# Matmuls whose result nobody reads at TensorE's waits, a merged last expert at the layer seam, and expert weights in 8 KB rows, in a two-layer hybrid MoE step

## The reference, cut to what matters

```python
def trunk_layer(x, cond, attend, p, w_router, router_bias):
    mod = jax.nn.silu(cond) @ p['w_ada'] + p['b_ada']
    sh1, sc1, g1, sh2, sc2, g2 = jnp.split(mod, 6, axis=-1)
    mix, k, v = mixer(modulate(x, p['norm1'], sh1, sc1), p, attend)
    x = x + g1 * mix
    h = modulate(x, p['norm2'], sh2, sc2)
    x = x + g2 * moe(h, w_router, router_bias, p['w_e_gate'], p['w_e_up'], p['w_e_down'])
...
def moe(h, w_router, router_bias, w_gate, w_up, w_down):
...
    # 16 experts in 4 groups; the best group, and its best 2 experts, are chosen for each token
    hid = jax.nn.silu(jnp.einsum('td,edf->tef', t, w_gate)) * jnp.einsum('td,edf->tef', t, w_up)
    hid = hid * combine.astype(hid.dtype)[..., None]
    return jnp.einsum('tef,efd->td', hid, w_down).reshape(B, L, D)
```

## Time and profile before

| | |
|---|---|
| median of 3 runs | 1215.33 us (1215.15 to 1216.3) |
| the profiled execution | 1213.5 us |
| its span (what the profile covers) | 1211.7 us |
| PE busy | 1114.1 us, 92% of the span |
| DVE, ACT, POOL busy | 699.8, 457.5, 58.0 us |
| chain that ended last, by engine | PE 68%, DVE 21%, ACT 4%, DMA 3%, issue 3% |
| mean granted TensorE clock | 0.971 of full speed |

### The profile page before, as it was taken

The page is one execution under the profiler, slowest core; times in us unless marked ns, Lnnn a source line. Parts: engine busy times, 40 slices in busy tenths (PEclk is TensorE's granted clock), DMA queues, the critical chain, the costliest instruction groups (busy, mean ns, idle before and its releaser), DMA issues.

```text
span 1211.7 us, 19456 instructions
## 1 busy us (share of the span) xinstructions
PE 1114.1 (92%) x6494; PEld 776.4 (64%) x6495; DVE 699.8 (58%) x1364; ACT 457.5 (38%) x827; POOL 58.0 (5%) x71
## 2 busy tenths in 40 slices
PE   3899999999898999999869999999998999999993
PEld 1798777678673455555459887776886655445551
DVE  0466999875632334445465799987654345234546
ACT  2443776443341122222254267645442222112224
POOL 1000000000100000000310000000000000000006
PEclk9999999999999999999979999999988999999996
DMA  8832655623798989999943446563058799989991
GB/s 316 272 109 104 215 206 209 239 72 105 296 395 314 345 312 395 393 394 395 386 134 107 141 170 235 201 218 115 3 187 301 272 392 394 392 278 395 395 374 54
DMA packets 138055, 309.93 MB, mean 256 GB/s; under 512 B 7953, under 2 KB 40113, under 8 KB 131329
## 3 DMA queue, kind: packets, MB, share of 16 engines
q1 hardware_dynamic: 134448, 302.25, 68.6%
q0 software_dynamic: 1472, 4.52, 1.0%
q10 hardware_dynamic: 2064, 2.22, 0.6%
HBM read 307.10 MB, written 1.87 MB: 255 GB/s over the span
## 4 chain that ended last, share of the span: by engine, by line
PE 68%; DVE 21%; ACT 4%; DMA 3%; issue 3%; DVEq 0%; SPq 0%; ACTq 0%
PE ps L772 15%; PE ps L805 11%; DVE conv L1878 7%; PE ps L775 6%; PE ps L859 5%; PE ps L906 3%; PE ps L1110 3%; PE ps L907 3%; PE ps L908 3%; PE ps L830 3%; DMA ring<-in_w_ada 2%; DVE w_lo L1894 2%; PE ps L831 2%; PE ps L1023 2%; PE ps L1025 2%
## 5 line engine op out<-in xcount | busy, mean ns | idle before, releaser
L1753 DVE SCALAR_TENSOR_TENSOR nat<-ps,weight,nat 128x512 f32<-128x512 f32 x180 | 124.1, 745 | 111.1 <-PE ps L831 111.1
L1878 DVE SCALAR_TENSOR_TENSOR conv<-ub,dw,conv 128x414 f32<-128x414 f32 x240 | 137.1, 645 | 0.1
L908 PE MATMUL ps<-h_hi,w_lo 128*128 128x384 f32 x384 | 130.4, 340 | 0.0
L1740 DVE TENSOR_TENSOR orow_lo<-ps,orow_hi 64x512 fp32r<-64x512 f32 (+1 forms) x64 | 44.1, 689 | 108.2 <-ACT orow_hi L1284 107.3
L772 PE MATMUL ps<-second,xgT 128*64 128x256 f32 x896 | 102.3, 381 | 0.0
L772 PE MATMUL ps<-ring,xgT 128*64 128x256 f32 x832 | 95.7, 381 | 1.4 <-DMA ring<-in_w_e_gate 1.0
L772 PEld LDWEIGHTS ps<-second,xgT 128*64 128x64 f32 x896 | 65.2, 137 | 39.0 <-issue 12.6
L906 PE MATMUL ps<-h_hi,gate_hi 128*128 128x384 f32 x256 | 90.0, 352 | 0.0
L907 PE MATMUL ps<-h_lower,gate_hi 128*128 128x384 f32 x256 | 87.1, 340 | 0.0
L772 PEld LDWEIGHTS ps<-ring,xgT 128*64 128x64 f32 x832 | 62.6, 137 | 36.5 <-issue 12.4
L1271 ACT ACTIVATE hidT<-ps 128x256 f32<-128x256 f32 (+1 forms) x32 | 13.4, 418 | 185.5 <-PE ps L790 185.5
(11 more groups left out here) (271 smaller groups left out, 2038.4 us busy)
## 6 DMA issues: line engine op xcount, KB each, us to landing
ring<-in_w_ada SPq DMA_DIRECT2D x48, 1024.0 KB, 7.4
second<-in_w_e_gate SPq DMA_DIRECT2D x32, 1024.0 KB, 11.7
second<-in_w_e_up SPq DMA_DIRECT2D x32, 1024.0 KB, 12.7
second<-in_w_e_down SPq DMA_DIRECT2D x32, 1024.0 KB, 11.7
ring<-in_w_e_gate SPq DMA_DIRECT2D x32, 1024.0 KB, 13.3
ring<-in_w_e_up SPq DMA_DIRECT2D x32, 1024.0 KB, 13.9
ring<-in_w_e_down SPq DMA_DIRECT2D x32, 1024.0 KB, 13.3
ring<-in_w_in SPq DMA_DIRECT2D x30, 1024.0 KB, 5.6
```

The source lines that it names most:

```text
L908: last = pe.matmul(ps[:, b, 0:T], lower[:, o:o + P], hi[:, k, 0:T], start=False, stop=(k == k_tiles - 1))
L1740: dve.tensor_tensor(orow_lo[a:z, o:o + 512], ps[a:z, 5 + h, :], orow_hi[a:z, o:o + 512].bitcast(F32), ALU.subtract).then_inc(fr[5 + h], 1)
L1753: dve.scalar_tensor_tensor(sums, ps[:, b, :], weight[:, t, bass.ds(at, 1)], sums, ALU.mult, ALU.add).then_inc(fr[b], 1)
L1878: dve.scalar_tensor_tensor(conv[:, i, :], src, w, conv[:, i, :], ALU.mult, ALU.add).then_inc(tapped, 1)
```

## The change

1. **Rows of 8 KB.** The expert weights' view is `(h p k) n` instead of `(k p) n`: partition p of a piece gets neighbouring rows of the matrix, one run of 8 KB. So that the products stay the same, the tokens are stored in the order that fits: ACT's `nat_hi` and DVE's `nat_lo` read PSUM in steps of 4 words, and DVE's `hid` reads silu (SBUF) and the up product (PSUM) in steps of 2 words.
2. **`stay_busy(b, n)`**: n bf16 matmuls of 128x512 into a bank, whose result nobody reads, ahead of a step that waits: 11 before `qkv` (layer 0), 5 before the first `scores`, 10 before `rank` (layer 1), 8 and 14 before `spread` (layers 0 and 1), and 2, 4 and 6 at the seam.
3. **Seam.** The body of expert 15 holds its last `back` and the question about overflow itself; one conditional jump and one jump are left. `n1` starts with banks 7 and 4.
4. **Order.** ACT's load of the sigmoid table (L1456) moves behind the modulation; `spread` does the three `nat_hi` products first, then the three of `nat_lo`; `lower_h(4)` moves behind the third pair of `place`.
5. In `add_routed` the factor 1.0 becomes a column of ones in SBUF.

```diff
-    ("n1", [0, 1, 7, 4, 0, 1]),
+    ("n1", [7, 4, 0, 1, 7, 4]),
...
+        def by_row(rows, t, h):
+            return rows[:, t, h * 512:(h + 1) * 512].rearrange("q (k p) -> q k p", k=4)
...
-        w_g = A["w_e_gate"].rearrange("l e (k p) n -> (l e) p k n", p=P)
+        w_g = A["w_e_gate"].rearrange("l e (h p k) n -> (l e) h p k n", h=2, p=P)
...
+            def stay_busy(b, n):
+
+                for _ in range(n):
+                    pe.matmul(ps[:, b, :], ones_b[:], ones_b[:].unsqueeze(1).to_broadcast([P, 4, P]), start=True, stop=True)
...
+                if l == 0:
+                    b, n = use("qkv", 0, l)
+                    begin(b, n)
+                    pe.wait_ge(consts2, 5)
+                    stay_busy(b, 11)
...
+                b, n = use("scores", 0, l)
+                begin(b, n)
+                stay_busy(b, 5)
                 scores(0)
...
-                pe.wait_ge(route_r, l + 1)
                 b, n = use("rank", 0, l)
                 begin(b, n)
+                if l + 1 == DEPTH:
+                    stay_busy(b, 10)
+                pe.wait_ge(route_r, l + 1)
...
+                        t, lower = i % NT, i // NT
+                        part = (nat_hi, nat_lo)[lower]
...
+                b, n = use("spread", 0, l)
+                begin(b, n)
+                hb, hn = use("h2n", 1, l)
+                pe.wait_ge(freed[hb], hn + 1)
+                stay_busy(b, 8 if l + 1 < DEPTH else 14)
...
+                                ahead = pe.mark_branch_hint_location()
+                                steps(small, before_narrow)
+                                last_back(small)
+                                pe.br_cond(over > 0, f"further{n}", f"usual{n}_{int(small)}")
+                                with nc.body(f"usual{n}_{int(small)}", valid_engines=[pe.engine]):
+                                    no_further()
+                                    pe.br(f"joined{n}").branch_hint(ahead)
...
+                    back(n_of, freed, full, small, range(0, 2))
+                    if l + 1 < DEPTH:
+                        stay_busy(3, 2)
+                    back(n_of, freed, full, small, range(2, NT), halves=(0,))
+                    if l + 1 < DEPTH:
+                        stay_busy(3, 4)
+                    back(n_of, freed, full, small, range(2, NT), halves=(1,))
...
+                    if l + 1 < DEPTH:
+                        stay_busy(3, 6)
...
-                act.activation(warm[:], eps[:], ACT.Sigmoid)
                 modulate("n2", 1, 1, l)
                 modulate("n2", 1, 2, l)
+                act.activation(warm[:], eps[:], ACT.Sigmoid)
...
-                    act.activation(nat_hi[:, t, h * 512:(h + 1) * 512], ps[:, b, :], ACT.Copy).then_inc(nat_hi_r, 1)
+                    act.activation(by_row(nat_hi, t, h), ps[:, b, :].rearrange("q (p k) -> q k p", k=4), ACT.Copy).then_inc(nat_hi_r, 1)
...
-                        dve.scalar_tensor_tensor(x_, routed[:, h, :], 1.0, x_, ALU.mult, ALU.add).then_inc(signal, 1)
+                        dve.scalar_tensor_tensor(x_, routed[:, h, :], ones[:, 0:1], x_, ALU.mult, ALU.add).then_inc(signal, 1)
...
-                dve.tensor_tensor(hid[:, 0:cols], silu[:, 0:cols], ps[:, 3, 0:cols], ALU.mult).then_inc(fr[3], 1)
+                    rows, pairs = "q (k p) -> q k p", "q (p k) -> q k p"
...
+                dve.tensor_tensor(hid[:, 0:cols].rearrange(rows, k=2, p=P), silu[:, 0:cols].rearrange(pairs, k=2, p=P),
+                                  ps[:, 3, 0:cols].rearrange(pairs, k=2, p=P), ALU.mult).then_inc(fr[3], 1)
...
-                        if half_at == 0 and t == NT - 1:
-                            lower_h(4)
...
-                        for i in (2, 3, 5):
+                        for i in (4, 2, 3, 5):
```

More of the change, by code:

```diff
@@ L817, in expert_parts, with back @@
                 return gate, up, turn_own, turn_hid, down
-            def back(n_of, fr, fs, small, tiles=range(NT), gate_bank=2):
+            def back(n_of, fr, fs, small, tiles=range(NT), gate_bank=2, halves=(0, 1)):
                 if 0 in tiles:
@@ L825, in back @@
                 for t in tiles:
-                    for h in range(2):
+                    for h in halves:
                         b, u = SUM_BANKS[2 * t + h]
@@ L1103, in spread @@
                     for i in range(2 * NT):
[L1104 to L1108, removed]
+                        t, lower = i % NT, i // NT
+                        part = (nat_hi, nat_lo)[lower]
+                        if half_at == 0 and k % 4 == 0:
+                            hi_ = H2N.index((t, k // 4))
+                            if lower:
+                                hb, hn = use("h2n", hi_, l)
+                                pe.wait_ge(freed[hb], hn + 1)
+                            else:
+                                pe.wait_ge(nat_hi_r, l * 6 + (hi_ + 1))
+                        if k == 0 and not lower:
                             pe.wait_ge(place_r, l * (2 * NT) + (half_at * NT + t + 1))
@@ L1130, in _, with expert @@
                 settle(pe)
-                def expert(e, before_e=None, in_second=False, turn=0, between=None):
+                def expert(e, before_e=None, in_second=False, turn=0, between=None, over=None):
                     if in_second:
@@ L1164, in steps @@
                         down(small)
-                    if before_e is None:
+                    if over is not None:
+                        narrow = pe.value_load(narrow_e[0:1, bass.ds(e, 1)], min_val=0, max_val=1)
+                        before_narrow = pe.value_load(narrow_e[0:1, bass.ds(before_e, 1)], min_val=0, max_val=1)
+                        n = next(forks)
+                        pe.br_cond(narrow > 0, f"small{n}", f"wide{n}")
+                        for small in (True, False):
+                            with nc.body(("wide", "small")[small] + str(n), valid_engines=[pe.engine]):
+                                ahead = pe.mark_branch_hint_location()
[5 more added lines that the diff above has]
+                                    pe.br(f"joined{n}").branch_hint(ahead)
+                        with nc.body(f"further{n}", valid_engines=[pe.engine]):
+                            further()
+                            pe.br(f"joined{n}")
+                        nc.switch_bb(f"joined{n}")
+                    elif before_e is None:
                         by_width(pe, e, steps)
@@ L1205, in further @@
                         back(lambda b: further_use(b, l, i), freed_o, full_o, False, range(NT), 5)
-                usual_or_over(pe, ahead, no_further, further)
+                expert(0, in_second=True, between=spread_rest)
+                with pe.Fori(0, NE // 2 - 1) as pair_:
+                    expert(pair_ * 2 + 1, pair_ * 2, False, pair_)
+                    expert(pair_ * 2 + 2, pair_ * 2 + 1, True, pair_ + 1)
+                over = pe.value_load(overfull[0:1, 0:1], min_val=0, max_val=1)
+                expert(NE - 1, NE - 2, False, NE // 2 - 1, over=over)
         @block.scalar
```

32 lines of the change are left out of this document (13 added, 19 removed).

## The result

The changed kernel took 1202.79 us (median of 4 runs, 1201.35 to 1203.38) where the kernel before took 1215.47: a ratio of 0.9913, with an interval from 0.9891 to 0.9935. The forecast was 1204.0. Its profiled execution took 1203.38 us, with a span of 1201.7, 10.0 us less than the span of before; it is the longest of the four.

A forecast was written before the change was run, and what follows sets the result against it. The kernel was taken as bound mostly by PE, with DVE's convolution next. Terms -1.5 - 1.3 - 2.7 + 1.3 - 2.4 - 4.7 - 0.6 + 0.6 = -11.3 us took 1215.33 to 1204.0; 8-in-10 range 1197 to 1211.

The forecast's parts named there:

- 8 KB rows, -1.5: Layer 0's expert 15: weights arriving faster in 8 KB runs remove PE's waits for gate and up, -1.5 us.
- Steps, 0: DVE's `hid` and `nat_lo`: stepped reads taken as 0 for `hid`; `nat_lo`'s +0.5 us a layer set off by moving `lower_h(4)`.
- Rival A: The steps cost: `hid` 0.5 ns an element longer, +4.8 us, so 1208.8 us; chance 0.22.
- `qkv`, -1.3: Layer 0's `qkv`: eleven fillers keep the clock, 16 products gain 1.7 us but can start 0.4 late, net -1.3 us.
- `spread` of layer 0, -2.7: Layer 0's `spread`: eight fillers fill PE's idle 1.9 us, so 44 products take 7.74 us instead of 10.48, -2.7 us.
- `rank`, +1.3: Layer 1's `rank`: ten fillers ahead of the wait are too many and start it 1.3 us later, +1.3 us.
- `spread` of layer 1, -2.4: Layer 1's `spread`: fourteen fillers fit a 3.99 us gap, then 16 steps run at full clock, -2.4 us.
- rival D: The fillers don't keep the clock, run at 0.44 us each and delay later steps: 1219.1 us, slower than before; chance 0.07.
- Seam, -4.7: Layer 0's seam: one jump gone, banks free early and transposes at full clock let `qkv` begin earlier, -4.7 us.
- Small parts: Table load leaving tile 1's chain, -0.3 us a layer, -0.6 together; column of ones in `add_routed`, 12 x 0.05, +0.6 us.
- Theory 1: The prediction's account: fillers hold the clock, merged body saves a wait for code, rows save the wait at expert 15.
- theory 2: Alternative tested in the experiments: the drops of the clock come by chance and the fillers do nothing.

The follow-up runs named there:

- changed again: The changed kernel with no edit, measured and profiled a second time: 1202.37 us against 1214.38 for before (ratio 0.9903).
- no fillers: The changed kernel with every stay_busy taken out: 1206.75 us (ratio 0.9942).
- rows only: The kernel before with the 8 KB rows and the steps that belong to them, nothing else: 1209.26 us (ratio 0.9959).
- better: Changed kernel with number 1.0, 18 fillers before layer 1's spread not awaiting lower_h, 17 for 6 at seam's end, 8 before the last back: 1200.62 us (0.988).
- that of the steps: The changed kernel plus ten unread tensor_tensor of 256 columns behind DVE's last instruction, in various SBUF and PSUM steps; no kernel time given.
- seam and order: The changed kernel without stay_busy, with old rows and the number 1.0, leaving merged body, banks and changed order: 1210.62 us (ratio 0.9966).

## Why the prediction was right, step by step

The forecast of 1204.0 lies 1.2 us over the median. The mechanisms of its main terms held, but that the number is so near is in part luck. In the first profile of the changed kernel the terms of the sum gained 13.1 us by lead (rows 2.1, `qkv` 1.5, `rank` 0, `spread` 3.5 and 1.8, seam 4.2), where they were put at 11.3; places that the sum doesn't have took back 5.0 (1.7 behind `logits` of layer 0, 1.5 at the jump into expert 1, 0.6 in `qkv` of layer 1, 1.2 at the end), and the rest gave some 2, so 10.0 were left. In the second profile 14.3 were left.

- **8 KB rows, -1.5.** Mis-sized: 2.1 us, in every kernel that has them (changed, changed again, no fillers, rows only, better) and 0.0 in those that don't. I had added up the named waits, which the view counts only from the end of the product before. From start to start the three steps of PE at these waits took 0.88, 1.05 and 0.84 us where the changed kernel has 0.39, 0.18 and 0.21, 2.0 us more. That the rows alone lie 5.2 us under before by median is not explained: the interval (0.9939 to 0.9979) allows 2.6, and none of the six executions under 1208 us, which had the higher granted clock, was profiled. It stays open.
- **Steps, 0.** Right, and shown. The value of `coef` was the right neighbour for `hid`. For `nat_lo` the neighbour `pair` was wrong: it reads SBUF in steps of 4, `nat_lo` reads PSUM, and the +0.5 us a layer was not there (683 ns and 682). Rival A would have come true with steps of 4 in SBUF: 27 x 0.18 us for the narrow experts alone. Two sayings of the Trainium skill part here. By the Trainium skill ("Vector Engine (DVE) Microarchitecture Reference", Measured stream behaviour on trn2) single words cost; that agrees at steps of 4 and 6 (0.60 us) and not at 2 (0.42). By the Trainium skill ("SBUF — State Buffer", Door 1) two words out of one line of 16 bytes are enough for full rate; that agrees with all three.
- **`qkv`, -1.3.** 1.5 in lead at the last `qkv`: the 16 products took 1.7 us less and began 0.19 us later (39.73 and 39.54), not 0.4, since the first product starts before the record of the last filler ends (37.36 + 2.53 = 39.89).
- **`spread` of layer 0, -2.7.** From `rank` to the last `spread` the changed kernel gains 3.5 us, in all four profiles with fillers in the table. But before itself gained 1.7 there in its second profile, and the other kernels without fillers 1.3 to 2.0. The fillers make sure of what otherwise comes sometimes and in part; against an average of the profiles without them they are worth some 2 us.
- **`rank`, +1.3.** Wrong as a fixed price: 0 in the first profile, where the ten fillers ended at 897.10 us and PE still waited until 898.38 for `chosen_b`. I had counted from one profile, in which `h2n` ran almost wholly at half clock (5.16 us, 2.82 in the first of the changed kernel). In six more profiles with these fillers `rank` began 0.06 to 0.31 us behind `chosen_b`, and 1.48 in that of the steps, where `h2n` took 5.36 us.
- **`spread` of layer 1, -2.4.** 1.8 from `rank` to the last `spread`, in both profiles of the changed kernel. The kernel without fillers gained 1.4 there too and the others without 0.9 or less, so against their average the fillers are worth some 1.4. The term missed that they wait for `lower_h` and start 1.0 us late; in the first profile they then ran in part at half clock, and the first `spread` came 1.6 us late by lead, which was rival D's mechanism at one of its sites.
- **Seam, -4.7.** 4.2 in the first profile and 5.0 in the second, from expert 15 to `qkv`. The part of the mechanism that is shown is that PE's wait reached beyond the data: in all ten profiles of the new seam 0.14 to 0.15 us are left behind `diag`, with fillers and without, where the old one had 0.9 to 4.7. The jumps as its whole cause are not shown. That the 4.7 us "are not a wait for data" was wrong for at least 0.66 of them, a wait for a bank: bank 0 came free only at 614.07, and tile 0 goes to banks 7 and 4 now. Against the other profiles of the old seam, which gained 1.1, 1.3 and (second profile of the rows) 3.3 by themselves, the change is worth nearer 3.
- **Small parts.** The table load gave about 0.4 us a layer by lead; the column's 0.06 us each is as predicted (0.05).
- **Left out.** The drop of the clock behind `logits` of layer 0: between the last `logits` and `rank` the lead falls from 2.0 to 0.3, though PE had no wait there. It isn't the change's doing, since before shows it too in its second profile. It goes against the premise of the fillers that the drop "follows a wait and never unbroken work": that was so in the rows shown, not in general.

Theory 1 stands, with 4.4 us for the fillers by median, 2.1 us by lead for the rows, and 3.8 us by median for seam and order; the share of the jumps in the last is open. Chance drops, as in theory 2, explain much of why single profiles of one kernel differ by up to 4 us, but not the medians.

## What to carry to other kernels

Compare two profiles by the lead of one engine, instruction by instruction, before a gain is put down to an edit, and take a second profile of the kernel before: a stretch at half clock in one profile may be absent in the next. Matmuls that nobody reads paid here where TensorE waits for some us and then works on; those that started late ran in part at the lower clock and were themselves waited for. At the seam a last body that holds what follows it, with banks that come free early, gained some 3 us. Before a wait is put down to a jump, look at when the bank that the next product writes comes free as well as at when its data does.

## What the runs showed of the hardware

- At `qkv` of layer 0 the 16 products behind eleven fillers ran at a granted clock of 1.00 (3.63 or 3.64 us) in all eight profiles that have them; behind a wait of 2.2 to 2.4 us they took 5.33 to 5.38 us in all six that don't.
- `h2n` behind `logits` ran at half clock for a part in 11 of the 14 profiles in layer 0 and in 11 in layer 1, though PE had no wait over 0.15 us in the products of 16 columns ahead of it. After the jump into expert 1, the gate took 7.13 us in five profiles and 8.5 to 10.2 in nine; a wait of 3.25 us was followed by 7.13 in one (before) and by 8.82 in another (seam and order).
- PE's wait at the old seam was 7.34, 7.14, 6.15 and 3.54 us in four profiles (two of before, two of the rows), whose seams have the same instructions; 4.06, 2.48, 1.49 and 0.25 us of it lay behind the freeing of bank 0. With the merged body, the new order of banks and no fillers it was 2.77 and 2.95, up to `diag`.
- DVE read PSUM in steps of up to 16 words in the time of steps of 1 (0.41 to 0.42 us for 256 columns), SBUF in steps of 2 (0.42 us) but not of 4 and 6 (0.60 us).
